# Bias rows stored shifted by partition, transposed value products for the small heads, and a router on feature blocks

## The reference, cut to what matters

```python
for l in range(DEPTH):                                  # DEPTH = 2
    z = rms_norm(x, norm_mix[l]) @ w_in[l]              # 1024 -> 2992 columns
    ya = diff_attention(...)   # 4 heads: softmax(m=0) - lam * softmax(m=1), values of 128, bias table_a
    yb = dsa_attention(...)    # 4 heads of 64, only the 64 best keys by an index score, bias table_b
    yc = mla(...)              # 4 heads of 64, no bias
    x = x + concat([ya, yb, yc]) @ w_out[l]
    x = x + hier_moe(rms_norm(x, norm_ffn[l]), ...)     # group, then 2 of 8 experts in it
return rms_norm(x, norm_final)

# the bias depends on the distance alone:
b = table[t5_bucket(s[None, :] - t[:, None])]
# a head's output:
o = einsum('bhqk,bkhd->bqhd', softmax(logits), v)
```

## Time and profile before

| | |
|---|---|
| median of 3 runs | 1207.34 us (1206.68 to 1208.55) |
| profiled execution, its own time | 1206.32 us |
| its span, first to last instruction | 1204.5 us |
| busy: PE, DVE, ACT, POOL | 1054.3, 344.7, 235.3, 18.0 us |
| HBM read | 442.63 MB |

### The profile page before, as it was taken

How to read it: one execution, slowest core, us unless ns; L and a number is a source line. 1 busy time by engine, 2 the same in 40 slices (tenths; PEclk the granted TensorE clock), 3 DMA queues, 4 the chain that set the end, 5 groups by cost and what they waited for, 6 DMA issues and landing times.

```text
span 1204.5 us, 18674 instructions
## 1 busy us (share of the span) xinstructions
PE 1054.3 (88%) x7889; PEld 594.6 (49%) x7892; DVE 344.7 (29%) x966; ACT 235.3 (20%) x578; POOL 18.0 (1%) x49
## 2 busy tenths in 40 slices
PE   9999999987887888778999999999887968787886
PEld 5777564443434343434468765554443434334433
DVE  3445563211111111111247365622111111111112
ACT  1234311111111111111112441121111111111112
POOL 1000100000000000000010000000000000000000
PEclk9999999998888889888999999999988988898899
DMA  8677579999999999999998056899999999999995
GB/s 303 218 278 280 227 271 429 426 427 426 426 428 424 429 425 427 426 427 427 414 389 309 26 221 254 318 426 428 426 426 426 428 425 427 425 425 427 425 429 214
DMA packets 59142, 446.00 MB, mean 370 GB/s; under 512 B 10888, under 2 KB 15536, under 8 KB 32176
## 3 DMA queue, kind: packets, MB, share of 16 engines
q1 hardware_dynamic: 57216, 443.57, 89.6%
q10 hardware_dynamic: 1840, 1.19, 0.3%
HBM read 442.63 MB, written 2.11 MB: 369 GB/s over the span
## 4 chain that ended last, share of the span: by engine, by line
PE 49%; DMA 44%; SPq 3%; DVE 2%; issue 1%; ACT 1%; POOL 0%; POOLq 0%; ACTq 0%; DVEq 0%
DMA ring<-in_w_up 39%; PE pv L1738 11%; PE pj L1396 8%; PE tr L1757 4%; PE pj L1637 4%; DMA arena<-in_w_up 4%; PE lg L1765 4%; PE pj L1765 3%; SPq L577 3%; PE pj L1402 2%; PE pj L1487 2%; PE tr L1725 1%; PE lg L1426 1%; PE pv L1749 1%; PE pj L1608 1%
## 5 line engine op out<-in xcount | busy, mean ns | idle before, releaser
L1738 PE MATMUL pv<-ring,xT 128*32 128x256 f32 x3136 | 287.7, 446 | 84.5 <-DMA ring<-in_w_up 52.2
L1738 PEld LDWEIGHTS pv<-ring,xT 128*32 128x32 f32 x3136 | 141.9, 123 | 188.2 <-issue 140.7
L1235 DVE TENSOR_SCALAR arena<-arena 128x128 f32<-128x128 f32 x64 | 14.5, 227 | 663.5 <-ACT arena L817 663.2
L1765 PE MATMUL lg<-arena 128*128 128x512 f32 x256 | 131.9, 597 | 0.0
L1765 PE MATMUL pj<-arena 128*128 128x512 f32 x256 | 130.7, 592 | 0.0
L656 ACT ACTIVATE arena<-pv 128x256 f32<-128x256 f32 x64 | 24.5, 383 | 512.2 <-PE pv L1738 512.2
L656 ACT ACTIVATE arena<-tr 128x512 f32<-128x512 f32 (+3 forms) x168 | 92.3, 558 | 125.1 <-PE tr L1757 107.0
L1738 PE MATMUL pv<-arena,xT 128*32 128x256 f32 x640 | 88.5, 434 | 19.6 <-DMA ring<-in_w_up 19.6
L1396 PE MATMUL pj<-xT,ring 128*128 128x256 f32 x448 | 100.6, 381 | 0.0
L1396 PEld LDWEIGHTS pj<-xT,ring 128*128 128x128 f32 x448 | 83.9, 190 | 12.9 <-issue 1.0
L1757 PE MATMUL tr<-ring,arena 128*32 128x512 f32 x696 | 84.2, 594 | 1.9 <-issue 1.9
(11 more groups left out here) (226 smaller groups left out, 933.2 us busy)
## 6 DMA issues: line engine op xcount, KB each, us to landing
ring<-in_w_up SPq DMA_DIRECT2D x48, 2048.0 KB, 38.8
ring<-in_w_gate SPq DMA_DIRECT2D x46, 2048.0 KB, 43.6
ring<-in_w_down SPq DMA_DIRECT2D x42, 2048.0 KB, 42.2
arena<-in_w_down SPq DMA_DIRECT2D x14, 2048.0 KB, 42.3
arena<-in_w_gate SPq DMA_DIRECT2D x12, 2048.0 KB, 46.0
ring<-in_w_in SPq DMA_DIRECT2D x10, 2048.0 KB, 20.0
arena<-in_w_up SPq DMA_DIRECT2D x8, 2048.0 KB, 38.1
ring<-in_w_out SPq DMA_DIRECT2D x4, 2048.0 KB, 16.2
```

The source lines that it names most:

```text
L1738: ins = mm(gu_ps[i * CAP:(i + 1) * CAP, :], xg[:, j, c:c + CAP], w, start=(j == 0), stop=(j == KD - 1), tile_position=(0, i * CAP), skip_g ...
L1765: ins = mm(acc[t][half], pgT[:, b, t, :], y[:, 512 * half:512 * half + 512], start=False, stop=last, skip_group_check=True)
```

## The change

1. **Bias.** The line is stored 128 times over (8 x 128 x 384 floats, 1.5 MB instead of 12 KB), and `load_bias` reads partition p from copy p at an offset that falls by one with p. The rows arrive in order, and `flips`, `flipped` and the loaded reversing matrix are gone. SP's `w_out` loads wait for the store to have landed, no longer for `flipped`; POOL's mask of the bias waits for the load.
2. **Values.** For kinds B and C `combine` multiplies the softmax weights by the reciprocal, and every `turn_p` waits for it. `values_pair` treats two steps (four heads) at once: the values are the stationary operand (64 columns, at column 0 or 64 of the array), the transposed weights the moving one (128 columns), and the result is already transposed. `finish_pair` copies it to `mixT_up`. The upper half of `turn_mix` and of `mixT` is gone, and `out_half` becomes `out_upper` (from `mixT_up`) and `out_lower` (from `xT`), each four matmuls, upper first.
3. **Router.** x is transposed by contiguous blocks of 128 features, the router weights are loaded in that order, `turn_xn` and `router` go by halves, the upper half of tile 1 before its lower half is added; the sum of squares of tile 1 is in two parts. SP loads the spare piece earlier.

```diff
-    lines_d = nc.dram_tensor("bias_lines", (8, LINE), F32, kind="Internal")
+    lines_d = nc.dram_tensor("bias_lines", (8, P * LINE), F32, kind="Internal")
...
+        mixT_up = rows[:, :, 512:].rearrange("p t (j s) -> p t j s", j=KD // 2)
+        xnT_up = zT_flat[:, 1024:2048].rearrange("p (t j s) -> p t j s", t=TOK, j=KD // 2)
...
-                    sp.wait_ge(flip_read, 4)
+                    sp.wait_ge(lines_out, 16)
...
-                    pool.wait_ge(flip_read, 4)
+                    pool.wait_ge(bias_in, 16)
...
-                act.dma_start(lines_d.ap(), lines).then_inc(lines_out, 16)
+                act.dma_start(bass.AP(lines_d, 0, [[P * LINE, 8], [LINE, P], [1, LINE]]), spread(lines, 1, P)).then_inc(lines_out, 16)
             def load_bias():
                 act.wait_ge(lines_out, 16)
-                act.dma_start(bias[:, 0:8, :], bass.AP(lines_d, 0, [[1, P], [LINE, 8], [1, SEQ]])).then_inc(bias_in, 16)
+                act.dma_start(bias[:, 0:8, :], bass.AP(lines_d, P - 1, [[LINE - 1, P], [P * LINE, 8], [1, SEQ]])).then_inc(bias_in, 16)
...
                     own.mark(v.reciprocal(rden[:, s % 4, :], den[:, s % 2, :]))
-                    if kind == "A":
-                        own.after()
+                    own.after()
+                    if kind != "A":
+                        both = prob[:, s % 2, 0:2 * n].rearrange("p (m k) -> p m k", m=2)
+                        v.tensor_tensor(both, both, spread(rden[:, s % 4, :], 2, n), ALU.mult).then_inc(mixed_p, 1)
...
+                def finish_pair(s):
+                    dve.wait_ge(pv_done, at(l, PV_USES, use_of(s) + 1))
+                    v.tensor_copy(mixT_up[:, t, o:o + 2, :].rearrange("p j s -> p (j s)"), pv[:, use_of(s) % 2, 0:2 * P]
+                                  ).then_inc(pv_read, 1)
...
                 add_half(0, 1)
+                finish(14); finish(15)
+                own.after()
+                dve.sem_inc(ssq_ready, 1)
                 mix_norm(1)
                 add_half(0, 0)
-                squares(0)
+                squares(0).then_inc(ssq_ready, 1)
                 own.mark(rows_half(0, 0))
                 own.mark(rows_half(0, 1))
                 add_half(1, 1)
+                own.mark(squares(1, 512, D_MODEL))
...
-                    if kind == "A":
-                        pe.wait_ge(mixed_p, at(l, 8, s - 7))
-                    else:
-                        pe.wait_ge(exped, at(l, NS, s + 1))
+                    pe.wait_ge(mixed_p, at(l, NS, s + 1))
...
+                def values_pair(s):
+                    pe.wait_ge(tr_read, at(l, TR_EV, 12 + s + 2))
+                    for m in range(2):
+                        for k in range(t + 1):
+                            for i in range(2):
+                                h = i + 2 * m
+                                ins = mm(bank[64 * i:64 * i + 64, m * P:(m + 1) * P], vv[:, k, 64 * h:64 * h + 64],
+                                         pT[:, (s + i) % 2, m * n + k * P:m * n + (k + 1) * P],
+                                         start=(k == 0), stop=(k == t), tile_position=(0, 64 * i), skip_group_check=True)
...
+                def out_upper(t, half):
+                    for k in range(KD // 2, KD):
+                        mm(pj[:, half], mixT_up[:, t, k - KD // 2, :], weights(6 + half)[:, k, :], start=(k == KD // 2), stop=False)
...
+                out_upper(0, 1)
                 turn_mix(0)
-                out_half(0, 1, 0, KD // 2)
                 turn_p(12); turn_p(13); logits(14)
-                out_half(0, 1, KD // 2)
+                out_lower(0, 1)
                 values(12); values(13)
+                out_upper(0, 0)
                 turn_p(14); turn_p(15); values(14); values(15)
-                out_half(0, 0, 0, KD // 2)
-                turn_mix(1)
-                out_half(0, 0, KD // 2)
+                out_lower(0, 0)
...
+                out_upper(1, 1)
+                turn_mix(1)
+                turn_xn(0, 0)
+                turn_xn(0, 1)
+                out_lower(1, 1)
+                router(0, 0, True)
+                router(0, 1, False)
+                out_upper(1, 0)
...
+                turn_xn(1, 1)
+                out_lower(1, 0)
+                router(1, 1, True)
+                turn_xn(1, 0)
                 pe.wait_ge(picked0, l + 1)
                 gather_first(0, 0, KD // 2)
-                turn_xn(1)
+                router(1, 0, False)
                 gather_first(0, KD // 2, KD)
```

More of the change, by code:

```diff
@@ L81 @@
 NS = len(STEPS)
-PJ_EV = 9 + 4 + 2
+PJ_EV = 9 + 4 + 1
 TR_EV = 2 + 8 + 2 + NS
@@ L804, in _ @@
                 for t in range(TOK):
[L805 to L808, removed]
+                    for i, half in enumerate(((0, 1), (1, 0))[t]):
+                        act.wait_ge(xnT_done, at(l, 4, 2 * t + i + 1))
+                        dst = xnT_up[:, t] if half == 1 else xT[:, 0:4, t * P:(t + 1) * P]
+                        copy(dst, (tr, pj)[t][:, half].rearrange("p (j s) -> p j s", j=4)).then_inc(xnT_read, 1)
                     act.wait_ge(gmax_ready, at(l, TOK, t + 1))
@@ new lines, in out_lower, with turn_xn @@
+                def out_lower(t, half):
+                    if t == 0:
+                        pe.wait_ge(pj_read, at(l, PJ_EV, PJ_EV))
+                    else:
+                        pe.wait_ge(mix_read, l + 1)
+                    for k in range(KD // 2):
+                        ins = mm(pj[:, half], xT[:, k, t * P:(t + 1) * P], weights(6 + half)[:, k, :],
+                                 start=False, stop=(k == KD // 2 - 1))
+                    ins.then_inc(wo_done, 1)
+                def turn_xn(t, half):
+                    pe.wait_ge(x_added, at(l, 4, 2 * t + 2 - half if t == 1 else 2))
@@ L1654, in router @@
+                    ins.then_inc(xnT_done, 1)
+                def router(t, half, first):
+                    pe.wait_ge(xnT_read, at(l, 4, 2 * t + (1 if first else 2)))
+                    if t == 0 and first:
                         pe.wait_ge(pv_read, at(l, PV_USES, PV_USES))
                         pe.wait_ge(wr_ready, l + 1)
-                    for j in range(KD):
-                        if j == KD // 2 and t == 0:
-                            pe.wait_ge(xnT_read, at(l, 3, 2))
-                        elif j == KD // 2:
-                            pe.wait_ge(xnT_upper, l + 1)
-                        ins = mm(pv[:, t, 0:R_COLS], xT[:, j, t * P:(t + 1) * P], wr[:, j, :],
-                                 start=(j == 0), stop=(j == KD - 1))
@@ L1663, in router @@
-                    ins.then_inc(router_done, 1)
+                    for j in range(4):
+                        src = xnT_up[:, t, j, :] if half == 1 else xT[:, j, t * P:(t + 1) * P]
+                        ins = mm(pv[:, t, 0:R_COLS], src, wr[:, 4 * half + j, :], start=first and j == 0, stop=not first and j == 3)
+                    if not first:
+                        ins.then_inc(router_done, 1)
+                out_upper(0, 1)
                 turn_mix(0)
-                out_half(0, 1, 0, KD // 2)
@@ L1905, with use_of @@
 WIDE = 2 * (2 + BODY)
-PV_USES = 3 + NS
+PAIRS = 4
+PV_USES = 3 + PAIRS + NS // 2
+def use_of(s):
+    return 3 + (s // 2 if s < 2 * PAIRS else s - PAIRS)
 def gather_use(q):
```

202 lines of the change are left out of this document (77 added, 125 removed).

## The result

The changed kernel takes **1226.57 us** (median of 4 runs, 1223.60 to 1228.94); the kernel before, measured beside it, 1207.01 (4 runs, 1205.38 to 1208.55). That is slower, as forecast, but 8.4 us above the predicted 1218.2 and outside the range of 1204 to 1224.

What follows compares the result with a forecast made beforehand. Weight stream bounds the expert rounds, PE the attention. Bias +8.9, clock +1.5 and both layers +0.5 make +10.9 us on 1206.32: 1217.2, and 1218.2 for the median, which lies 1.0 higher; range 1204 to 1224.

Steps and rivals of the forecast that it cites:

- the 2.5 us before `turn_p(13)`: Mixing, each layer: PE waits because `exp(13)` stands behind ACT's copy of `turn_mix(0)`; 2.5 us lost.
- a wait of about 1 us at `turn_p(6)` and `turn_p(7)`: Values, each layer: PE waits for DVE's new multiplication of the softmax weights; 0.95 us lost.
- the landing T: Layer 0 bias: the store lands at T = 55.2, q and k transposes start at T + 17.9; 8.9 us lost.
- 1.5 for the clock: Layer 0, PE work behind the bias stop: low clock costs 1.5 us, within bounds of none and 7.6.
- 10.4 x 1.5 x 2: Bias store: the bias load's 10.4 us scaled for 1.5 times the bytes and half the engines; 31.2 us.
- the first rival: Bias store: eight engines, only the moving part grows; 22.9 us, T = 46.9, total 1208.5 us; chance 0.25.
- The rule of the ports: Bias store: partitions 0 to 7 reach two ports at 27.2 GB/s each; 29 us behind its start, 1219.6 us total.
- +0.25 us each: Each layer: values, mixing and router terms, -1.2 + 0.95 - 0.8 - 1.1 - 0.4 + 2.5 + 0.3, sum to +0.25 us.
- the stop of 12 us at the bias: Layer 0: PE stands some 12 us while ACT waits for the store, then runs at a low clock.
- its own sign: Test of the prediction: wrong if layer 1 attention changes by over 1.5 us or the bias load issues before 46 us.
- the third rival: Values' column halves do not overlap (1222.2 us), or the store nears its upper bound (every 10 us add 10); chance 0.13.
- a store beyond 37 us: Bias store: a case left outside the range of 1204 to 1224, with most of the fast case.

Runs made afterwards that it cites:

- bias_undone: The changed kernel with its bias part undone (small store, flips on PE): 1209.11 us, ratio 1.0026 against the kernel before.
- kept_warm: The changed kernel with SP issuing the bias load and PE doing ten products of zeros before `turn_p(13)`: 1202.27 us, ratio 0.9972 against the kernel before.
- wide_store: The changed kernel with the 1.5 MB store reading all 128 partitions, eight copies from each, in another DRAM order: 1207.53 us, ratio 1.0008 against the kernel before.
- apart9: The changed kernel with head lines on 16 partitions each and the store reading eight partitions 9 apart: 1214.88 us (one run).

## Why the prediction was right and where it was wrong

**The direction and the places were right.** ACT's wait for the store, DVE and PE behind it, the 2.5 us before `turn_p(13)`, a wait of about 1 us at `turn_p(6)` and `turn_p(7)`: all are in the trace. The pair of products is within the 0.12 to 0.18 us that were foreseen. The way from the landing T to the transposes of q and k was T + 17.9 with 1.5 for the clock, 19.4; it measured 79.55 - 60.23 = 19.3.

**The store was mis-sized.** The prediction took 31.2 us, T = 55.2; it was 36.1, T = 60.2: **5.0 us** of the miss. The step that failed is "10.4 x 1.5 x 2": the row of the bias load scaled by bytes and by the share of engines. By that step eight partitions are eight partitions. Apart they take 23 us, about the first rival's 22.9; the 13 us on top come from their being neighbours. That the sum came as near as 31.2 is in part luck, since it doubled the start too and had no term for the neighbours. The rule of the ports was at hand in the prediction, with 29 us behind the start. Added to the start of 3.7 that the first rival reads from the same rows it makes 33; in the trace the first packet moved some 4 us after the issue and the rest took 32 us, 49 GB/s in place of 54. It was weighed and then not used for the sum. By it the sum would have been the 1219.6 us that the prediction gives, 1.4 more.

**The layers were mis-sized by the clock.** Forecast were +0.25 us each, measured +2.06 and +2.04: **3.6 us** of the miss. The terms of work and waiting were good: without a fall of the clock a layer is at +0.41 (bias_undone, layer 0; kept_warm) or +0.61 (kept_warm, layer 1). But the prediction charged the stop of 12 us at the bias for the clock and not the one of 2.5 us in each layer. The step that failed is the sum of a layer, "+2.5" for `turn_p(13)` with nothing for the work behind it: it named the wait and left out what the wait does to that work, 1.7 and 1.4 us here. By its own sign, a change of more than 1.5 us in layer 1, the prediction was wrong there.

The smaller terms. A pair product: 0.15 forecast; the eight of `values_pair(2)` take 1.02 us from start to start (113.10 to 114.12), 0.13:

```profile
113.10 1.09 PE L1451 MATMUL pv<-arena 128*64 128x128 f32 x16
114.12 0.66 PE L1436 MATMUL tr<-con,arena 128*128 128x128 f32 x4
...
120.91 0.66 PE L1436 MATMUL tr<-con,arena 128*128 128x128 f32 x4 [0.83 <-DVE arena L1064]
122.17 0.66 PE L1436 MATMUL tr<-con,arena 128*128 128x128 f32 x4 [0.60 <-DVE arena L1064]
```

The gain was smaller all the same, since the old products took 0.21 to 0.22 from start to start and not the 0.25 read from the earlier trace rows: pairs 0 and 2 gave 1.0 us in layer 0, not 1.2. The wait for the multiplication, 0.83 + 0.60 against 0.42 before, cost 1.0, as forecast (0.95). The first half of the third rival, that the column halves do not overlap, is out; its second half, a store towards its upper bound, is what happened, by half of the 10 us that it names. The two sizes above make 8.6 of the 9.0 us between the predicted sum (1217.2) and the profiled execution (1226.25); the rest is in stretches that the change does not touch, which differ by about 1 us from one execution to another.

**The range** ended at 1224 with the sentence that a store beyond 37 us lies outside. The store did not go beyond it, so the range had to hold the result by its own words; it failed because no case in it had the fall of the clock twice more. The store alone would have made 1223.2.

## What to carry to other kernels

Ask of every DMA wait which engine stands at it, and what else that engine serves: the same store of 36 us cost 20 us behind ACT and nothing behind SP, which had to wait there anyway. Count the partitions of a small source by where they lie, and by how many engines they feed when other loads share these: neighbours took 36 us, separate ones 23, all 128 took 14. Where an edit leaves PE standing for some 2.5 us, charge for the matmuls behind the wait as well, between nothing and the 3.2 us seen here, and look first for an instruction on the producing engine that can go ahead of the copy in its way.

## What was not expected of the hardware

- The same idle of 2.57 us was followed by the full clock (1.00) in layer 0 of bias_undone and in both layers of wide_store, and by the low one (0.50) in layer 1 of bias_undone, with 0 to 3.2 us lost. With ten bf16 products of zeros in the idle it was 1.00 in both layers. What decides between the cases was not settled.
- A packet of 1.5 KB held its DMA engine 0.165 us when its source was one of eight neighbouring partitions and 0.065 us when these lay 17 apart. While the store of the changed kernel ran alone with the last weight chunks (56 to 60 us), the eight engines that carried it moved 118 GB/s together.
- Eight partitions 17 apart or 9 apart gave the same (22.98 and 22.87 us): each of their eight engines passed a packet of the store every 0.14 us, as did each of the sixteen in wide_store.
- The store from neighbours passed 104 packets in its first 2 us and later 29 to 32 a us. Why it began faster was not settled.
- A table of 16 KB in 512 packets of 32 B in place of one of 1 KB, loaded beside x, came with a start of the program later by 2.0 us (wide_store) to 3.6 us (apart9).
